# Neighborhood attention spread over the chunks of its own projections, with one preloaded bias table

## The reference, cut to what matters

```python
q, k, v = jnp.split(h @ w_qkv, 3, axis=-1)
q = rmsnorm(q.reshape(grid), q_g)          # per head, over its 64 channels
k = rmsnorm(k.reshape(grid), k_g)
...
s = jnp.einsum('bnqhd,brnkhd->bhnqrk', q_r, k_r).astype(jnp.float32) * scale
bias = rpb[:, dr_idx[None, None, :, None], dc_idx[:, :, None, :]]   # by row and column distance
s = jnp.where(mask, s + bias.astype(jnp.float32)[None], neg)
p = jax.nn.softmax(s.reshape(s.shape[:4] + (wr * NA_SPAN,)), axis=-1)
...
o = jnp.einsum('bhnqrk,brnkhd->bnqhd', p, v_r)
return o.transpose(1, 0, 2, 3).reshape(bsz, seq, d) @ w_out
```

## Time and profile before

| | us |
|---|---|
| median of 3 runs | 2352.57 (2347.67 to 2354.16) |
| profiled execution: its time | 2362.4 |
| profiled execution: its span | 2360.6 |
| neighborhood layer's mixer, first chunk to last transpose | 238.9 |

### The profile page before, as it was taken

One profiled execution on the slowest core, in us unless ns is written; L12 is line 12 of the kernel. 1 busy time (PEld: TensorE's weight loads), 2 busy tenths in 40 slices (PEclk: granted clock), 3 DMA queues, 4 the chain that ended last, 5 costly groups with the idle time before them and its releaser, 6 DMA issues.

```text
span 2360.6 us, 34355 instructions
## 1 busy us (share of the span) xinstructions
PE 2138.7 (91%) x13674; PEld 1911.1 (81%) x13674; DVE 1419.0 (60%) x1565; ACT 926.2 (39%) x996; POOL 21.1 (1%) x53
## 2 busy tenths in 40 slices
PE   7997659899999989999997789999788899998999
PEld 7996538777777789999994479989667799898998
DVE  4576575667666566556643345667666556656565
ACT  3344242556555543333432343335211233334332
POOL 0000000000000000000000000000000000000000
PEclk8998879899999989999996689999799999999999
DMA  6633202477677645455553425557200255544553
GB/s 188 221 126 107 81 13 60 167 282 299 248 268 276 221 158 177 146 194 179 177 164 33 71 73 193 180 194 223 72 0 0 87 181 180 193 161 156 183 188 114
DMA packets 258690, 368.06 MB, mean 156 GB/s; under 512 B 29210, under 2 KB 233069, under 8 KB 246253
## 3 DMA queue, kind: packets, MB, share of 16 engines
q1 hardware_dynamic: 258605, 366.85, 46.8%
HBM read 365.78 MB, written 1.05 MB: 155 GB/s over the span
## 4 chain that ended last, share of the span: by engine, by line
PE 58%; DVE 11%; DMA 5%; ACT 5%; issue 3%; DVEq 0%; ACTq 0%; POOL 0%
PE proj L830 28%; PE acc L1020 9%; PE proj L845 7%; DMA raw<-in_w_exp_up_dram 5%; PE proj L1201 2%; DVE ring_lo L2324 2%; DVE ring_lo L1789 2%; PE acc L1171 2%; PE acc L1266 1%; PE acc L1267 1%; PE acc L1311 1%; ACT ring_hi L1643 1%; ACT second_hi L1643 1%; ACT ring_hi L1437 1%; PE acc L1324 1%
## 5 line engine op out<-in xcount | busy, mean ns | idle before, releaser
L1789 DVE TENSOR_TENSOR ring_lo<-raw,ring_hi 128x2048 fp32r<-128x2048 f32 x242 | 554.6, 2293 | 279.9 <-ACT ring_hi L1437 279.7
L1437 ACT ACTIVATE ring_hi<-raw 128x2048 fp32r<-128x2048 f32 x242 | 462.4, 1912 | 634.0 <-PE proj L830 336.4
L830 PE MATMUL proj<-g_hi,ring_hi 128*128 128x256 f32 x1408 | 396.9, 282 | 7.1 <-DVE hid L2106 7.1
L830 PE MATMUL proj<-g_hi,ring_lo 128*128 128x256 f32 x1408 | 395.6, 281 | 0.0
L830 PE MATMUL proj<-g_lo,ring_hi 128*128 128x256 f32 x1408 | 395.5, 281 | 0.0
L830 PE MATMUL proj<-h_hi,ring_hi 128*128 128x256 f32 x1232 | 354.8, 288 | 17.9 <-DVEq L1825 9.5
L830 PE MATMUL proj<-h_lo,ring_hi 128*128 128x256 f32 x1232 | 352.3, 286 | 0.0
L830 PE MATMUL proj<-h_hi,ring_lo 128*128 128x256 f32 x1232 | 352.1, 286 | 0.0
L830 PEld LDWEIGHTS proj<-g_hi,ring_hi 128*128 128x128 f32 x1408 | 266.3, 189 | 9.5 <-issue 7.8
L830 PEld LDWEIGHTS proj<-g_lo,ring_hi 128*128 128x128 f32 x1408 | 266.3, 189 | 1.6
L830 PEld LDWEIGHTS proj<-g_hi,ring_lo 128*128 128x128 f32 x1408 | 266.3, 189 | 0.0
(11 more groups left out here) (401 smaller groups left out, 3480.3 us busy)
## 6 DMA issues: line engine op xcount, KB each, us to landing
raw<-in_f_w_dram SPq DMA_DIRECT2D x132, 1024.0 KB, 5.0
raw<-in_w_exp_gate_dram SPq DMA_DIRECT2D x32, 1024.0 KB, 4.8
raw<-in_w_exp_up_dram SPq DMA_DIRECT2D x32, 1024.0 KB, 5.0
raw<-in_w_exp_down_dram SPq DMA_DIRECT2D x32, 1024.0 KB, 4.8
raw<-in_w_in_dram SPq DMA_DIRECT2D x29, 1024.0 KB, 5.1
raw<-in_a_w_in_dram SPq DMA_DIRECT2D x24, 1024.0 KB, 5.1
raw<-in_b_w_qkv_dram SPq DMA_DIRECT2D x12, 1024.0 KB, 5.1
raw<-in_c_w_in_dram SPq DMA_DIRECT2D x12, 1024.0 KB, 5.1
```

The lines of the kernel that those rows point to most:

```text
L830: last = pe.matmul(pair(s.slot)[:, a, :], w[:, k, a * P:(a + 1) * P], h[:, k, :], start=(k == 0 and w is hi and h is h_h and (a == 0 or no ...
L1437: act.activation(w_hi[n.slot][:, :], raw[n.slot][:, :], ACT.Copy).then_inc(hi_ready, 1)
L1789: dve.tensor_tensor(w_lo[n.slot][:, :], raw[n.slot][:, :], w_hi[n.slot][:, :].bitcast(f32), SUB)\
```

## The change

- The weight stream is reordered: q and k chunks alternate (`b_q0`, `b_k0`, `b_q1`, ...), then the four v chunks. A chunk brings two head pairs.
- The steps of attention are no longer a loop behind the projections. They are written out one by one on each engine, on PE between the two halves of a chunk (`middle`) or between chunks. The projections use two PSUM banks in turn; the third (`na_side`) is for the sums of squares and the spread of k's norm.
- q isn't normalized: DVE multiplies the scores by q's inverse norm, which is a column (`rate`) since queries stand on partitions, in the instruction that adds the bias. POOL makes the inverse norms by a power.
- The bias is loaded once for all heads into `na_bias` (16 heads x 6 rows of 64): 32 DMAs of 64 x 6 runs of 256 bytes, issued after the first round of `ffn0`'s loads. POOL adds the mask to the whole table in one instruction.
- q's columns are reversed within each grid row when they are drained, so that scores and bias agree. The probabilities are turned back by a product with `flip` (plain fp32, N = 128), which also transposes them, in place of a transpose.
- `na_out` begins its first two chunks without the last two tiles of its operand.

```diff
-          ("b_q", 4), ("b_k", 4), ("b_v", 4), ("na_out", 4), ("ffn1", MLP_CHUNKS),
+          ("b_q0", 1), ("b_k0", 1), ("b_q1", 1), ("b_k1", 1), ("b_q2", 1), ("b_k2", 1), ("b_q3", 1), ("b_k3", 1), ("b_v0", 1), ("b_v1", 1), ("b_v2", 1), ("b_v3", 1),
+          ("na_out", 4), ("ffn1", MLP_CHUNKS),
...
+            def load_bias():
+                sp.wait_ge(drained, DRAINED["a_out0"] + 1)
+                rpb = A["b_rpb_2"]
+                head, row = (2 * NA_ROWS - 1) * (2 * NA_COLS - 1), 2 * NA_COLS - 1
+                for h in range(HEADS):
+                    for half in range(2):
+                        src = bass.AP(rpb.tensor, h * head + (NA_SPANS - 1 - half) * row + NA_COLS - GRID_W,
+                                      [[1, GRID_W], [row, NA_SPANS], [1, GRID_W]])
+                        dst = na_bias[half * GRID_W:(half + 1) * GRID_W, h, :]
+                        sp.dma_start(dst.rearrange("p (a b) -> p a b", b=GRID_W), src).then_inc(bias_loaded, 16)
...
                     load(Chunk(c + 2, g), down(i), 2)
+                    if isinstance(i, int) and i == 0 and after_first:
+                        after_first()
...
+            def sums(j):
+                pe.wait_ge(q_squared, j + 1)
+                pe.wait_ge(k_squared, j + 1)
...
+                            last = pe.matmul(na_side[:, c:c + 2], square[:, a, t * P:(t + 1) * P], headones[:, 0:P:HD],
+                                             start=True, stop=True)
+            def k_spread(j):
+                pe.wait_ge(qk_rated, j + 1)
...
+                            last = pe.matmul(na_side[h * HD:(h + 1) * HD, c:c + P],
+                                             rate[:, j, 1, t, 2 * a + h:2 * a + h + 1].to_broadcast([P, HD]), ident[:, :],
+                                             start=True, stop=True)
+            def score(i):
+                pe.wait_ge(k_normed, i // 2 + 1)
...
                 for t in range(TT):
+                    for h in range(2):
+                        r = slice(h * HD, (h + 1) * HD)
+                        last = pe.matmul(acc[:, h, t * SEQ:(t + 1) * SEQ], pj[r, i, t * P:(t + 1) * P], pj[r, KT + i, :],
                                          start=True, stop=True)
+            def turn_probs(i):
+                pe.wait_ge(na_weighed, i + 1)
...
+                            last = pe.matmul(acc[:, 2 + h, kt * SEQ + t * P:kt * SEQ + (t + 1) * P],
+                                             na_probs[i % 2][:, h, t * SEQ + kt * P:t * SEQ + (kt + 1) * P], flip[:, :],
+                                             start=True, stop=True)
...
+                project_na("b_q2", product_f, False, lambda: (sums(1), score(1)))
+                k_spread(1)
+                turn_probs(0)
+                project_na("b_k2", product_f, False, lambda: score(2))
+                turn_probs(1)
+                project_na("b_q3", product_f, False, lambda: (sums(2), score(3)))
+                k_spread(2)
+                turn_probs(2)
+                project_na("b_k3", product_f, False, lambda: score(4))
+                turn_probs(3)
...
+                    bias = na_bias[:, :, :].rearrange("p h (s c) -> p (h s) c", c=GRID_W)
+                    pool.tensor_tensor(bias, bias, na_mask[:, :].unsqueeze(1).to_broadcast([P, HEADS * NA_SPANS, GRID_W]), ADD)\
+                        .then_inc(bias_masked, 1)
...
+            def keep(i):
+                act.wait_ge(na_probs_turned, i + 1)
...
+                act.activation(na_turned[i % 6][:, :, :], acc[:, 2:4, :], ACT.Copy).then_inc(na_kept, 1)
...
+            def k_norm(j):
+                dve.wait_ge(k_spread_out, j + 1)
+                k = pj[:, KT + 2 * j:KT + 2 * j + 2, :].rearrange("p a n -> p (a n)")
+                dve.scalar_tensor_tensor(out=k, in0=k, scalar=qk_gain[:, 0:1], in1=na_side, op0=MUL, op1=MUL).then_inc(k_normed, 1)
+            def score_rows(i):
...
+                        dve.scalar_tensor_tensor(out=na_probs[b][:, h, t * SEQ:(t + 1) * SEQ], in0=acc[:, h, t * SEQ:(t + 1) * SEQ],
+                                                 scalar=rate[:, i // 2, 0, t, i % 2 * 2 + h:i % 2 * 2 + h + 1], in1=na_bias[:, 2 * i + h, c:c + SEQ],
+                                                 op0=MUL, op1=ADD).then_inc(na_biased, 1)
```

559 lines of the change are left out of this document (358 added, 201 removed).

## The result

| | before | after |
|---|---|---|
| median, us | 2351.25 (2347.67 to 2354.16, 4 runs) | 2288.44 (2287.67 to 2291.83, 4 runs) |
| profiled execution: time / span, us | 2362.4 / 2360.6 | 2287.73 / 2286.0 |
| forecast, us | | 2333 (2298 to 2380) |

The ratio is 0.9739 with a 95% interval of 0.9715 to 0.9763: the change is worth 62.8 us, and the forecast had 19.3.

A forecast was written before the change was run, and what follows sets the result against it. The prediction took the layer to lose by TensorE's idle time and lowered clock, with no engine full in the attention loop. A 46.3 us layer gain less 27 in `ffn0` gave -19.3, from 2352.6 to 2333 us, range 2298 to 2380.

The forecast's parts named there:

- scores: TensorE in the layer: 32 score products, 20.2 us at most or 10.1 if two run together; the middle, 15.1, taken.
- spread of k's norm: TensorE in the layer: 32 products of N = 128 onto half the columns, between 3.4 and 13.6 us; 6.4 taken.
- Part 1, turning: TensorE's work in the layer at full clock, 159.1 us; in it 64 turning products at 0.42 each, 27.1 us.
- Part 2, the clock: Layer: 122.0 us of half chunks and fp32 groups granted 0.85 of the clock, costing 21.5 us more.
- The v chunks before are the nearest mix: Layer's clock: four v chunks with four fp32 groups between them, 44.20 us at 0.85, taken for the new mix.
- Part 3, the waits: Layer: TensorE waits 2.9 us for k's norm before three scores, 9, plus some 3 elsewhere: 12 us.
- count as nothing too: Layer: POOL's powers for the rates come between two TensorE steps and were given no cost.
- Part 4, `ffn0`: In `ffn0`: 32 bias DMAs at 1.5 us, 48, delay the sixth chunk's weights; 25.5 us stall plus 1.6 clock, 27.
- I count nothing: In `ffn0`: POOL's mask, up to 14.8 us, was given no cost because VectorE has slack; up to about 12 otherwise.
- The clock did not stay low: Rival, layer: half chunks and fp32 groups granted only 0.61, the 122.0 us become 200; time 2384 us; chance 0.20.
- the bias was not hidden: Rival, `ffn0`: bias DMAs move as fast as issued, so the sixth chunk is in time; 2306 us; chance 0.20.
- it did not come out even: Rival, `ffn0`: stall at its upper end with POOL holding up VectorE, -46 + 44, so 2351 us; chance 0.08.

The follow-up runs named there:

- the repeat: The changed kernel, unchanged, profiled in another execution: the layer took 164.7 us at a clock of 0.93, against 158.4 at 0.98.
- turn_twice: The changed kernel with each of the 64 turning products issued twice: 2296.26 us, layer 173.2 us.
- scores_apart: The changed kernel with the four products of a score ordered by head first, so only the middle two alternate row halves: 2285.90 us.
- sums_twice: The changed kernel with each of the 32 sums of squares issued twice: 2293.58 us, layer 171.0 us.
- steps_behind: The changed kernel with all twelve chunks first and the attention steps behind them, none between chunks: 2327.58 us, layer 201.1 us.
- before_shift: The kernel before with one small column made 16 wide instead of 2, moving everything allocated behind it by 32 bytes: 2328.51 us.
- mask_one: The changed kernel with POOL's mask added to the first head's part of the bias table only: 2275.18 us, `ffn0` 206.9 us.

## Why the prediction was wrong, step by step

**Direction and place** were right: faster, by the layer, at a price in `ffn0`. The size of the layer's gain was wrong: 80.2 against 46.3. By its parts:

| term of the layer, us | forecast | measured, by busy times (to about 1 us) |
|---|---|---|
| chunks | 92.2 | about 91.5, the rest of the busy time |
| sums, values, transposes | 18.3 | 18.5 |
| scores | 15.1 | 9.0 at full clock |
| turning | 27.1 | 15.9 |
| spread of k's norm | 6.4 | 4.4 |
| lower clock | 21.5 | 3.0 (9.9 in the repeat) |
| waits | 12 | 16.1 |
| layer | 192.6 | 158.4 |

**Part 1, turning.** "Between N = 2 (0.218) and N = 256 (0.63) a line gives 0.42" failed. The upper point was not a product of N = 256 in a row of its kind but one that alternated with another shape; in a row it takes 0.27 with 64 rows. A product of N = 128 costs 0.23 by `turn_twice`, hardly more than one of N = 2. It was to be "dearer than before and is the largest new cost": 11 us of the error are here. 6 more are in the scores, whose upper price came from the same row, and 2 in the spread, a middle between two ends. Together that is 19 us, as much as the clock. That two scores of different heads run together is not shown, since their order made no difference; 9.0 us were measured for all scores. The Trainium skill's "TensorE: Matmul & The Clock Gate", Part 3, has matmuls on different row groups run together, from which the prediction estimated 10.1; `scores_apart` gives no support to that being the cause. The Trainium skill's "TensorEngine Tiling (Array Packing)", Key Properties, has a change of the tiling mode drain the engine. Of that the trace shows little: the first full matmul behind four scores starts 0.31 us after the last of them, in place of 0.21 from one to the next, and its own successor 0.22 later in place of 0.12. Behind the turning products, which use the full array, that last distance is 0.20 as well.

**Part 2, the clock,** is the single term that failed most: 0.85 for 122 us, 21.5 us, where 3.0 were lost. "The v chunks before are the nearest mix" took one row for the rule. `sums_twice` shows what made most of that row: long groups of sums, which the change cuts in halves. What little was lost came from elsewhere: all of it lies behind the waits of part 3, which the forecast had added as a term of their own, with no clock in it. That interleaving keeps the clock up was right in size: `steps_behind` falls to 0.67 without it. In the repeat the clock cost about 10 us, so even there the forecast was at double.

**Part 3, the waits.** "`score(2)` waits 2.9; so do `score(4)` and `score(6)`" was right: 3.03 each, released by k's norm. The waits for POOL's rates, 5.7 us, were to "count as nothing too": the power of 16 columns takes 2.90 us and begins 1.1 us behind the sums, and the half chunk beside both takes 3.1.

**Part 4, `ffn0`.** 27 us forecast; against `before_shift`, which has the same pace, `ffn0` grew by 25.8. The sum was right by luck, since two terms were wrong and cancelled. The DMAs were nearer to the price by DMA: from the landing of the weight in front, 5 us after 958.25, to 1001.0, they took 37.8 us, 1.18 each, not 1.5. With 37.8 for 48 the forecast's own chain gives a stall of 15.3 us, and `mask_one` waited 15.8. POOL's mask, "I count nothing", cost 8.2: VectorE had slack, but a rest beside POOL's mask was not slowed by a share. In both profiles it ended 2.2 us behind the mask, so it stood still for as long as the mask still ran.

**The rivals.** The clock did not stay low; the bias was not hidden; it did not come out even. The fault was common to all four cases: each took its fp32 prices from the same rows, and none went below 2298.

**Not in the forecast at all:** the MLPs' pace. It gives some 10 us (3.2 to 4.4 each in `ffn0`, `ffn2` and `ffn3`, less 1.5 in `ffn1`, which had moved to h). With the layer's 34 that is about the 43.5 us by which the medians miss the forecast. The two profiles differ by 12 us more than the medians, of which 8.3 lie in the first stage, whose code is the same.

## What to carry to other kernels

A price read from a row belongs to its neighbours too: a product that alternates with another shape, or a chunk behind one certain group, is not the price of the product or the clock of "the mix". Look for a second row with other neighbours, or keep both ends open. Small dependent steps laid between the half chunks of a full engine are worth more than their own time, since the chunks cover the waits, and the clock was higher too (together some 40 of 80 us here). And a forecast of waits should not be kept apart from that of the clock: here a wait of 2 to 3 us had up to 2.9 us of lost clock behind it. Before a large instruction is given to POOL, look at what VectorE does at that moment, and cut it.

## What the runs showed of the hardware beyond that

- POOL's `tensor_tensor` over 6144 fp32 columns (13.2 to 13.4 us) held a VectorE instruction of 2.29 us for 10.51 and 15.10 us, until 2.2 us behind its own end; in eight pieces of 768 it cost `ffn0` nothing.
- The same matmuls at full granted clock ran at four paces, 96 of them in 11.07, 11.43, 11.47 or 11.67 us, and kept one through an MLP but for one case; moving g and all that is allocated behind it by 32 bytes was worth 20 us of 2350. Twice the pace was another at the same place: open.
- The same layer, with the same waits, had a mean clock of 0.98 or 0.93 in different executions, 6 us apart. Each stretch of lower clock began behind a wait of 2.2 to 3.2 us.
- Plain fp32 products with N = 2 and N = 128 cost the same, 0.22 and 0.23 us, 0.11 for each record.
- A POOL power of 128 x 16 took 2.90 us.
